# Attention of the sample streams moved from a stage of its own into the two gate projections

## The chip, the cores and the metric

The kernel runs on one core of one Trainium2 chip, written in Bass with every semaphore set by hand. The metric is device time in microseconds from start to end of one execution.

## The reference, cut to what matters

One layer of a hybrid encoder: half-step feed-forward, a token mixer, half-step feed-forward, final norm. There are 1024 tokens of one new stream (prompt) and 8 running streams of 16 new tokens (sample), so T = 1152 tokens of width 1024. The mixer is what changes:

```
xr, gr, q, k, v, fl, ga, gb = split(h @ w_in)
a_out = gelu(gr) * rg_lru(causal_conv(xr))
logf  = log_sigmoid(fl + b_fgt)
att   = attend(q, k, v, logf)     # prompt: causal. sample: over cache and new tokens
z = sigmoid(ga) * (a_out @ w_br_rnn) + sigmoid(gb) * (att @ w_br_att)
x = x + (1 + gate) * (z @ w_out)

def fox_sample(...):              # 8 streams, 16 heads of 64, 1024 cached rows + 16 new
    s = einsum('bqhd,bkhd->bhqk', q, kk) * HEAD_DIM ** -0.5
    s = s + ft[query] - ft[key]   # ft: running sums of logf, past ones and new
    return einsum('bhqk,bkhd->bqhd', softmax(where(mask, s, -inf)), vv)
```

The outputs are the tokens after the layer, and the new keys, values, logf and states.

## The kernel before, in words

Each engine has its own program, a row of stages: setup, first feed-forward, projection (`proj_*`), recurrent branch (`brr_*`), prompt attention (`att_*`), sample attention (`sat_*`), merge of the branches and output projection (`merge_*`), second feed-forward, final norm. Loops are hardware loops (`Fori`) whose bodies are written out in full; the first and last passes are often written out ahead of and behind the loop.

A product of full precision is three fp32r passes (`mm3`, L273 to L277): weights and activations are each split into a high part (ScalarE, L257, and a cast) and the remainder (GpSimd, L263, for weights). A weight block is 1024 x 256. SyncE loads it, ScalarE and GpSimd split it, TensorE uses it for six groups (two tiles of 128 outputs, three chunks of 384 tokens); a group is eight steps over k of three matmuls into one PSUM bank. `PROJ_SLOTS` and the like say which buffers a block takes and how many blocks ago they were used last.

The projection has four iterations of seven blocks, for the columns xr, gr, q, k, v, ga, gb; groups rotate over six banks, which ScalarE empties. Between the groups of v and ga, TensorE turns keys and values to token rows (L1109) for the outputs. Between those of q it does the small products of the recurrence gates (L1132), whose recurrence VectorE computes. Gate values and q, k, recurrent output go to DRAM. The recurrent branch loads its 4.7 MB input at once, splits it in three chunks (ScalarE L1438, VectorE L1453) and starts.

The sample attention (`sat_*`) has 16 units, a stream times half of the heads, eight heads in four pairs. For one unit: load 2 MB of cached keys (`kc`) and 2 MB of values (`vc`), biases (`sp`, eight DMAs of 65 KB), new queries and keys in a scattered pattern of 16 tokens (`qd`, `kn`, L1730 and L1731). For each head pair, 8 transposes of keys (L1771) into banks 6 and 7, copies to `kTs` (ScalarE L1845, VectorE L1882), then two products of the pair's 32 query rows with 512 keys each (L1784). A pair writes 32 partitions of the score banks. Then new-token scores (L1792, L1794), reduction with the biases (L1888), Exp (L1849), nine transposes (L1804), copies (L1856, L1858, L1901), 36 products with the values (L1815) in rotation over the four pairs, scaling (L1904), a transpose (L1821), and the hi/lo split into the activations (L1917, L1921). Two units overlap: scores of the next one stand before the finish of the last one. The prompt attention ends with transposes at L1561; the merge starts with `mm3` matmuls as soon as the attention is in the activations.

Of the kernel before, what the change touches and what calls it, by code (L numbers as in the profile page):

```python
# [35 lines left out]
CH = 384  # L36
# [22 lines left out]
def program(nc, ctx, a, o):  # L59
# [101 lines left out]
    gate_p = sb(rnnf, "gate_p", [128, 2, 3])  # L161
    rnnf.close()
    brrf = ExitStack()
    a_stage = sb(brrf, "a_stage", [128, KT, T])
    state_out = sb(brrf, "state_out", [36, D])
    lf16 = sb(brrf, "lf16", [ST, 128])
    brrf.close()
    projf.close()
    set2.close()

# [24 lines left out]
    satf = ExitStack()  # L195
    NEWK = PAST // 128
    kc = [sb(satf, f"kc{n}", [128, NEWK, 512]) for n in range(2)]
    vc = sb(satf, "vc", [128, NEWK, 512])
    kTs = [sb(satf, f"kTs{n}", [128, PAST]) for n in range(2)]
    kn = [sb(satf, f"kn{n}", [128, 4, ST]) for n in range(2)]  # L200
    vn = [sb(satf, f"vn{n}", [ST, 512]) for n in range(2)]
    qd = [sb(satf, f"qd{n}", [128, 4, 2 * ST]) for n in range(2)]
    sp = [sb(satf, f"sp{n}", [128, PAST + ST]) for n in range(2)]
    spT = sb(satf, "spT", [128, NEWK + 1, 128])
    sstat = sb(satf, "sstat", [128, 2, 4])
    o_rows = sb(satf, "o_rows", [128, 128])
    satf.close()


# [16 lines left out]
    N_PROJ = 28  # L226
    B_BRR = B_PROJ + N_PROJ
# [5 lines left out]
    PROJ_SLOTS = [(0, 1, 2, 3), (1, 2, 0, 2), (0, 2, 1, 3), (1, 2, 2, 3), (0, 2, 0, 3), (1, 2, 1, 3), (0, 2, 0, 2)]  # L233
    BRR_SLOTS = [(0, 1, 2, 3), (1, 2, 1, 3), (0, 2, 0, 3), (1, 2, 1, 2)]
# [5 lines left out]
    BRR_RAWS = (PROJ_RAWS[0] + 16, PROJ_RAWS[1] + 12)  # L240
# [228 lines left out]
    def setup_tensor(eng):  # L469
# [5 lines left out]
        eng.sem_inc(sem("sa_sc"), 5)  # L475
# [568 lines left out]
    COLS = (COL_XR, COL_GR, COL_Q, COL_K, COL_V, COL_GA, COL_GB)  # L1044
    XR, GR, Q, K, V, GA, GB = range(7)
    ST_BEFORE = {Q: 0, K: 1, V: 2, GA: 2, GB: 3}
# [6 lines left out]
    def proj_sync(eng):  # L1053
        w_in_v = kview(a["w_in"][0])

        def load(i, j):
            load_block(eng, B_PROJ + i * 7 + j, PROJ_SLOTS[j], w_in_v[:, :, ds(i * 256 + COLS[j], 256)])

# [14 lines left out]
        for j in range(2, 7):  # L1073
            load(0, j)
        with eng.Fori(1, N_IT) as i:
            load(i, 0)
            eng.wait_ge(sem("ri_full"), i * 12)
            load_gates(i)
            for j in range(1, 7):
                load(i, j)  # L1080

    def proj_tensor(eng):
# [9 lines left out]
        def body(i, first):  # L1092
            for j in range(7):
                for n in range(6):
                    t, c = n // 3, n % 3
                    g = i * 42 + j * 6 + n
# [610 lines left out]

    UNITS = 2 * SB  # L1710

    def sat_sync(eng):

# [456 lines left out]
```

## Time and profile before

| | |
|---|---|
| three runs | 3626.4, 3628.4, 3630.88 us, median 3628.4 |
| profiled execution | 3627.85 us, span 3625.7 us, mean TensorE clock 0.975 |
| TensorE busy | 3439.9 us, 95% of the span |
| VectorE, ScalarE, GpSimd busy | 1283.6, 910.2, 704.2 us |
| DMA | 343.2 MB, mean 95 GB/s |

The span runs from the first instruction to the last. A busy TensorE need not be at its full rate: the granted clock is 1.00 or 0.50, and 32-row products run side by side or not while both count as busy. In the timelines a run of instructions of one line is merged into one row with its start, its length and its count; the last instruction of a run overlaps the next run, so starts are to be compared and not ends. An fp32 product is recorded as two matmuls, a transpose as one.

### The profile page before, as it was taken

What the parts mean: (1) busy time and instruction counts of PE and PEld (TensorE: products, weight loads), DVE (VectorE), ACT (ScalarE), POOL (GpSimd) and SP (SyncE); (2) the same over time, 40 slices, a digit from 0 to 9 for tenths busy, and PEclk for the clock granted to TensorE, in tenths of its full rate; (3) what the DMA queues carried; (4) which work ended last, traced back from release to release, by engine and by line L of the source; (5) the groups of instructions that cost most, each with busy time, mean ns of one, the idle gap of its engine ahead of it and who ended that gap; (6) DMA issues with size and microseconds to landing.
All of it is one profiled execution on the core that took longest, in us unless ns stands there. A gap on an engine that the chain in (4) does not pass through costs nothing.

```text
span 3625.7 us, 54412 instructions
## 1 busy us (share of the span) xinstructions
PE 3439.9 (95%) x21295; PEld 3232.4 (89%) x21295; DVE 1283.6 (35%) x2835; ACT 910.2 (25%) x1360; POOL 704.2 (19%) x283
## 2 busy tenths in 40 slices
PE   5999999999999999999988998888999999999997
PEld 3999999999889999999988886445998999999996
DVE  5322222233364141414116775332415322233225
ACT  3111111111233232323216663221113111111112
POOL 1222222222112112112212220000122222232220
PEclk7999999999999999999999999998999999999999
DMA  6232222221112222122443435997310111111101
GB/s 207 82 104 93 93 93 81 81 93 36 76 39 93 82 88 88 65 99 72 168 143 95 98 88 155 279 277 251 123 47 27 44 58 35 35 43 38 58 12 52
DMA packets 264224, 343.20 MB, mean 95 GB/s; under 512 B 56381, under 2 KB 201205, under 8 KB 263858
## 3 DMA queue, kind: packets, MB, share of 16 engines
q1 hardware_dynamic: 237682, 308.42, 27.4%
q10 hardware_dynamic: 26432, 33.18, 2.6%
q8 instruction: 86, 1.41, 0.2%
q14 instruction: 24, 0.20, 0.0%
HBM read 293.54 MB, written 48.01 MB: 94 GB/s over the span
## 4 chain that ended last, share of the span: by engine, by line
PE 88%; DVE 4%; DMA 3%; issue 2%; ACT 2%; SPq 1%; DVEq 0%; ACTq 0%
PE psum L273 25%; PE psum L277 25%; PE psum L276 24%; PE psum L1554 3%; DMA kn<-k_t 2%; PE psum L1784 2%; PE psum L1534 2%; PE psum L1771 1%; PE psum L455 1%; DVE h_f L660 1%; PE psum L1132 1%; PE psum L1521 1%; PE psum L1815 1%; SPq L1738 1%; PE psum L1522 1%
## 5 line engine op out<-in xcount | busy, mean ns | idle before, releaser
L273 PE MATMUL psum<-acts_hi,w_hi 128*128 128x384 f32 x4032 | 1375.9, 341 | 50.3 <-DVE past_rows L309 25.2
L277 PE MATMUL psum<-acts_hi,w_lo 128*128 128x384 f32 x4032 | 1358.7, 337 | 0.0
L276 PE MATMUL psum<-acts_lo,w_hi 128*128 128x384 f32 x4032 | 1358.4, 337 | 0.0
L273 PEld LDWEIGHTS psum<-acts_hi,w_hi 128*128 128x128 f32 x4032 | 762.0, 189 | 71.6 <-issue 56.0
L263 POOL TENSOR_TENSOR w_lo<-w_raw,w_hi 128x2048 fp32r<-128x2048 f32 x106 | 492.1, 4650 | 1628.5 <-ACT w_hi L257 1628.5
L276 PEld LDWEIGHTS psum<-acts_lo,w_hi 128*128 128x128 f32 x4032 | 762.3, 189 | 3.3
L277 PEld LDWEIGHTS psum<-acts_hi,w_lo 128*128 128x128 f32 x4032 | 761.6, 189 | 0.0
L938 DVE TENSOR_TENSOR u_f<-psum,gated 128x384 f32<-128x384 f32 x132 | 73.6, 557 | 1045.2 <-ACT gated L884 1045.2
L971 DVE SCALAR_TENSOR_TENSOR x<-psum,mods,x 128x384 f32<-128x384 f32 (+1 forms) x552 | 314.6, 570 | 190.7 <-PE psum L277 190.7
L257 ACT ACTIVATE w_hi<-w_raw 128x2048 fp32r<-128x2048 f32 x106 | 200.6, 1911 | 639.7 <-PE psum L273 605.3
L273 PE MATMUL psum<-u_hi,w_hi 128*128 128x384 f32 x1056 | 355.3, 336 | 0.0
L277 PE MATMUL psum<-u_hi,w_lo 128*128 128x384 f32 x1056 | 354.9, 336 | 0.0
L276 PE MATMUL psum<-u_lo,w_hi 128*128 128x384 f32 x1056 | 354.7, 336 | 0.0
L907 POOL TENSOR_TENSOR u_lo<-u_f,u_hi 128x384 fp32r<-128x384 f32 x132 | 134.2, 1016 | 941.5 <-ACT u_hi L886 941.5
L884 ACT ACTIVATE gated<-psum 128x384 f32<-128x384 f32 x132 | 64.8, 491 | 914.8 <-PE psum L277 914.8
L273 PEld LDWEIGHTS psum<-u_hi,w_hi 128*128 128x128 f32 x1056 | 198.5, 188 | 0.3
L276 PEld LDWEIGHTS psum<-u_lo,w_hi 128*128 128x128 f32 x1056 | 198.5, 188 | 0.3
L277 PEld LDWEIGHTS psum<-u_hi,w_lo 128*128 128x128 f32 x1056 | 198.5, 188 | 0.0
L1554 PE MATMUL psum<-vh,pT 128*128 128x64 f32 x1152 | 147.2, 274 | 9.0 <-DVE acts_lo L1675 6.3
L1554 PEld LDWEIGHTS psum<-vh,pT 128*128 128x128 f32 x1152 | 141.4, 195 | 13.1 <-DVE acts_lo L1675 9.2
L1187 ACT ACTIVATE st<-psum 128x384 f32<-128x384 f32 x120 | 58.9, 491 | 334.3 <-PE psum L277 333.3
L1601 ACT ACTIVATE pr<-pr,stat 128x128 f32<-128x128 f32 (+7 forms) x128 | 98.8, 772 | 51.1 <-DVE stat L1655 50.0
(231 smaller groups left out, 2842.9 us busy)
## 6 DMA issues: line engine op xcount, KB each, us to landing
w_raw<-in_ffn_w SPq DMA_DIRECT2D x66, 1024.0 KB, 5.3
kc<-in_cache_k SPq DMA_DIRECT2D x16, 2048.0 KB, 10.9
vc<-in_cache_v SPq DMA_DIRECT2D x16, 2048.0 KB, 9.1
w_raw<-in_w_ada SPq DMA_DIRECT2D x28, 1024.0 KB, 5.0
w_raw<-in_w_in SPq DMA_DIRECT2D x28, 1024.0 KB, 5.2
sp<-sample_bias SPq DMA_DIRECT2D x128, 65.0 KB, 6.9
ada_w<-in_w_ada SPq DMA_DIRECT2D x4, 2048.0 KB, 15.5
w_raw<-in_w_ada_f SPq DMA_DIRECT2D x8, 1024.0 KB, 5.5
```

The lines of the kernel that those rows point to most:

```text
L257: eng.activation(w_hi[st][:], w_raw[raw][:], ACT.Copy).then_inc(sem("w_hi_done"), 1)
L263: eng.tensor_tensor(w_lo[st][:], w_raw[raw][:], w_hi[st][:].bitcast(F32), ALU.subtract).then_inc(sem("w_lo_done"), 1)
L273: pass1 = eng.matmul(out, whi, ahi, start=first, stop=False)
L276: eng.matmul(out, whi, alo, start=False, stop=False)
L277: return eng.matmul(out, wlo, ahi, start=False, stop=last)
L907: eng.tensor_tensor(u_lo[:, t, tokens_of(c)], u_f[n % 2][:], u_hi[:, t, tokens_of(c)].bitcast(F32), ALU.subtract).then_inc(sem("u_lo_done" ...
L938: eng.tensor_tensor(u_f[n % 2][:], ps[2 * (n % 2) + 1][:, 0:CH], gated[n % 2][:], ALU.mult).then_inc(sem("u_free"), 1)
L971: last = eng.scalar_tensor_tensor(xt[:, d, t0:t0 + cp], bank[:, 0:cp], mods[:, gate, d, 0:1], xt[:, d, t0:t0 + cp], ALU.mult, ALU.add)
L1534: last = eng.transpose(ps[4 + kb // 4][:, 128 * (kb % 4):128 * (kb % 4) + 128], pr[k % 4][:, 128 * kb:128 * kb + 128], ident[:])
L1554: last = eng.matmul(ps[6 + k % 2][:, 0:HD], pT[k % 2][:, 128 * kb:128 * kb + 128], vh[hh][:, kb, :], start=(kb == 0), stop=(kb == qi))
L1601: eng.activation(pr[k % 4][:, 0:keys], pr[k % 4][:, 0:keys], ACT.Exp, bias=stat[:, k % 4, 1:2], accum_out=stat[:, k % 4, 2:3]).then_inc(se ...
L1784: last = eng.matmul(psum[rows, base + 512 * bk:base + 512 * bk + 512], qd[g][:, p, :], kTs[p % 2][:, 512 * bk:512 * bk + 512], start=True, ...
```

## The change

- The projection keeps five blocks an iteration (xr, gr, q, k, v), with new buffer slots. Its value transposes move from the ga block to the xr block of the next iteration.
- The eight gate blocks (ga, gb of each quarter) become a stage of their own, `mix_*`, with 48 groups rotating over four banks. The other four banks are for the sample attention: three for scores, weighted values and output, one (`TURNED`) for turned keys.
- The 16 units are cut into pieces, 12 slots each. Three groups make a window; a slot comes every two k steps. In a window TensorE does slots 0 to 3 (turn keys of the first 512 rows, a head pair each), 4 and 5 (turn the last unit's probabilities), 6 (scores of the first half, four pairs one behind another), 7 to 10 (turn the second half's keys; slot 7 also the weighted values of the last unit, slot 9 its output transpose), 11 (scores of the second half, new tokens). The last body holds five windows in its twelve groups, with a slot every 1.5 steps.
- Keys, values, scores and biases have one buffer each, keys loaded in halves. `sp` and `spT` are single. Queries and new keys of all units are loaded once (`qs`, `kns`) and copied into place by GpSimd. ScalarE and VectorE share the key copies one by one.
- The attention goes to `att_s` and is split into the activations beside the prompt attention. The new tokens' offsets (`lf16`, `new_f`) are computed at the start of the new stage.
- The recurrent branch's input is loaded in three chunks and its first two are split behind the last groups. `sat_*` goes.

The core of the diff (the projection's part is the renumbering of blocks and waits from seven to five):

```
-    PROJ_SLOTS = [(0, 1, 2, 3), (1, 2, 0, 2), (0, 2, 1, 3), (1, 2, 2, 3), (0, 2, 0, 3), (1, 2, 1, 3), (0, 2, 0, 2)]
+    PROJ_SLOTS = [(0, 1, 2, 2), (1, 2, 1, 2), (0, 2, 0, 3), (1, 2, 2, 3), (0, 2, 1, 3)]
+    WINDOWS = 4
+    SLOTS = 12
+    def slots_of(n, last):
+        steps = [s * 3 // 2 if last else 2 * s for s in range((WINDOWS + last) * SLOTS)]
+        return [s for s, at in enumerate(steps) if 8 * n <= at < 8 * n + 8], steps
...
+        def window(i, w, begin=False, end=False):          # SyncE, mix_sync
+            u, b, g, _ = unit_of(i, w * SLOTS)
+            _, b1, g1, _ = unit_of(i, (w + 1) * SLOTS)
+            if w == 0:
+                load_block(eng, B_MIX + 2 * i + 1, ...)
+            if w == 2 and not end:
+                load_block(eng, B_MIX + 2 * i + 2, ...)
...
+            if not last_unit:
+                eng.wait_ge(sem("sa_kt"), u * 8 + 4)
+                keys(b1, g1, 0)
+            if not begin:
+                eng.wait_ge(sem("sa_pt"), u * 2)
+                bias(b, g)
+                eng.wait_ge(sem("sa_pv"), u)
+                values(b, g)
+            if not last_unit:
+                eng.wait_ge(sem("sa_kt"), u * 8 + 8)
+                keys(b1, g1, 1)
...
+            new_values(b, g)
...
+        def turn_keys(u, x, first):                        # TensorE, mix_tensor
+            half, p = x // 4, x % 4
+            if p == 0:
+                eng.wait_ge(sem(f"kc_loaded{half}"), u * 16 + 16)
+            if not (first and x == 0):
+                eng.wait_ge(sem(("sa_kev_v", "sa_kev_a")[x % 2]), u * 4 + (x + 1) // 2)
+            for m in range(4):
+                last = eng.transpose(ps[TURNED][:, 128 * m:128 * m + 128], kc[:, 4 * half + m, 128 * p:128 * p + 128], ident[:])
+            last.then_inc(sem("sa_kt"), 1)
+        def scores(u, g, half, first):
+            eng.wait_ge(sem("sa_kev_a"), u * 4 + 2 * half + 2)
+            eng.wait_ge(sem("sa_kev_v"), u * 4 + 2 * half + 2)
...
+            for p in range(4):
+                last = eng.matmul(psum[32 * p:32 * p + 32, base + 512 * half:base + 512 * half + 512], qd[g][:, p, :],
+                                  kTs[:, p, :], start=True, stop=True)
...
+        def piece(i, s, first, last):
+            if keys and at < 4:
+                turn_keys(u, at, first and s < SLOTS)
+            if done and at == 4:
+                turn_probs(u - 1, (0, 1, 2, 3, 8))
+            if done and at == 5:
+                turn_probs(u - 1, (4, 5, 6, 7))
+            if keys and at == 6:
+                scores(u, g, 0, first and s < SLOTS)
+            if keys and at >= 7 and at < 11:
+                turn_keys(u, at - 3, False)
+            if done and at == 7:
+                weighted(u - 1)
+            if done and at == 9:
+                turn_out(u - 1)
+            if keys and at == 11:
+                scores(u, g, 1, False)
+                new_scores(u, g, first and s < SLOTS)
+        def body(i, first=False, last=False):
+            for n in range(12):
+                here, steps = slots_of(n, last)
...
+                if first and n < 3:
+                    turn_tokens(eng, 12 * N_IT - 6 + 2 * n, 2 * n, 5)
+                    turn_tokens(eng, 12 * N_IT - 6 + 2 * n + 1, 2 * n + 1, 5)
...
+                for k in range(KT):
+                    for s in here:
+                        if steps[s] == 8 * n + k:
+                            piece(i, s, first, last)
+                    opens = mm3(eng, ps[n % 4][:, 0:CH], ...)
...
+        def piece(i, s, first, last):                      # ScalarE, mix_scalar
+            if keys and at in (0, 2, 7, 9):
+                eng.activation(kTs[:, x % 4, :], ps[TURNED], ACT.Copy).then_inc(sem("sa_kev_a"), 1)
+            if done and at == 1:
+                eng.activation(sp[:], sp[:], ACT.Exp, ...).then_inc(sem("sa_exp"), 1)
+            if done and at == 4:
+                eng.activation(spT[0:ST, NEWK, :], psum[0:ST, base + 1024:base + 1152], ACT.Copy)
+            if done and at == 5:
+                eng.activation(spT[:, 4:8, :], ...).then_inc(sem("sa_pe_a"), 1)
+        def body(i, first=False, last=False):
+            for n in range(12):
+                if first and n < 3:
+                    move_tokens(eng, N_IT - 1, 1, 2 * n, 5)
+                    move_tokens(eng, N_IT - 1, 1, 2 * n + 1, 5)
+                for s in here:
+                    piece(i, s, first, last)
+                eng.activation(st[t][:, tokens_of(c)], ps[n % 4][:, 0:CH], ACT.Sigmoid).then_inc(sem("proj_free"), 1)
+                if c == NC - 1:
+                    eng.dma_start((ga_dram, gb_dram)[j][...], st[t][:])
+                if n == 1:
+                    split_hi(eng, B_MIX + 2 * i + 1, ...)
+                if n == 7:
+                    split_hi(eng, B_MIX + 2 * i + 2, ...)
+                if last and n >= 9:
+                    a_hi(eng, n - 9)
...
+        def body(i, first=False):                          # GpSimd, mix_gpsimd
+            for w in range(WINDOWS):
+                if not (first and w < 2):
+                    eng.wait_ge(sem("sa_sc"), u * 2 - 2)
+                eng.tensor_copy(kn[g][:], kns[:, 4 * g:4 * g + 4, toks])
+                for half in range(2):
+                    eng.tensor_copy(qd[g][rows, :, ST * half:ST * half + ST], qs[rows, 4 * g:4 * g + 4, toks])
+                if w % 2 == 1:
+                    split_lo(eng, B_MIX + 2 * i + 1 + w // 2, PAIR_SLOTS[1 - w // 2])
...
+        def piece(i, s, first, last):                      # VectorE, mix_vector
+            if keys and at in (1, 3, 8, 10):
+                eng.tensor_copy(kTs[:, x % 4, :], ps[TURNED]).then_inc(sem("sa_kev_v"), 1)
+            if done and at == 4:
+                eng.tensor_copy(spT[:, 0:4, :], ...).then_inc(sem("sa_pe_v"), 1)
+                eng.reciprocal(old[:, 3:4], old[:, 2:3])
+            if done and at == 8:
+                eng.tensor_scalar(o_rows[:], psum[:, base + 1280:base + 1408], old[:, 3:4], None, ALU.mult)
+            if done and at == 10:
+                output(i, s // SLOTS - 1, u)
+            if keys and at == 11:
+                eng.tensor_tensor_reduce(sp[:], psum[:, base:base + PAST + ST], sp[:], 1.0, -3e38, ALU.add, ALU.max, new[:, 0:1])
+                eng.tensor_scalar(new[:, 1:2], new[:, 0:1], -1.0, None, ALU.mult).then_inc(sem("sa_neg"), 1)
...
+    def a_hi(eng, c):
+        eng.wait_ge(sem(f"a_loaded{c}"), 16)
+        eng.activation(acts_hi[:, :, tokens_of(c)], a_stage[c][:], ACT.Copy).then_inc(sem("a_hi"), 1)
...
     def att_scalar(eng):
+        eng.wait_ge(sem("br_full"), 24)
+        eng.activation(acts_hi[:, :, TP:T], att_s[:], ACT.Copy).then_inc(sem("sa_hi"), 1)
```

## Rows read from the trace of the kernel before

**Rows 1.** The page: busy tenths of TensorE in 40 slices of the span.
```profile
PE   5999999999999999999988998888999999999997
```

**Rows 2.** By stage: window, length, busy of each engine, clock, DMA share, GB/s.
```profile
1403.00:1592.00 189.00, 186.41 (x1062) 182.48 (x1062) 57.77 (x58) 57.85 (x85) 32.42 (x7) 1.00 0.25 84
...
2228.00:2515.00 287.00, 241.81 (x2224) 137.64 (x2224) 98.58 (x240) 70.36 (x128) 0.00 (x0) 0.93 0.87 262
```

**Rows 3.** The chain of waits in the sample attention: start, length, what.
```profile
2369.80 9.62 DMA kn<-k_t
```

**Rows 4.** Timeline of TensorE at both ends of the sample attention.
```profile
2223.02 0.47 PE L1561 MATMUL psum<-ident,att 128*128 128x128 f32 x1 [0.23 <-DVE att L1664]
...
2513.83 0.33 PE L1821 MATMUL psum<-ident,o_rows 128*128 128x128 f32 x1 [0.55 <-DVE o_rows L1904]
2515.20 0.44 PE L273 MATMUL psum<-acts_hi,w_hi 128*128 128x384 f32 x1 [1.04 <-DVE acts_lo L1921]
```

**Rows 5.** TensorE at the recurrent branch's start; then that stretch by windows.
```profile
1778.69 0.34 PE L277 MATMUL psum<-acts_hi,w_lo 128*128 128x384 f32 x1
1786.70 0.66 PE L273 MATMUL psum<-acts_hi,w_hi 128*128 128x384 f32 x1 [7.67 <-issue]
...
1786.50:1795.00 8.50, 8.30 (x33) 8.33 (x34) 7.19 (x4) 5.84 (x3) 3.38 (x1) 0.66 0.68 220
```

**Rows 6.** Timeline of TensorE in one unit of the sample attention.
```profile
2386.11 1.90 PE L1784 MATMUL psum<-kTs,qd 128*32 128x512 f32 x4
2387.95 1.09 PE L1771 MATMUL psum<-ident,kc 128*128 128x128 f32 x8
2388.97 2.30 PE L1784 MATMUL psum<-kTs,qd 128*32 128x512 f32 x8
2391.20 0.27 PE L1792 MATMUL psum<-causal_r,pick_r 16*128 16x16 f32 x1
...
2391.59 1.20 PE L1804 MATMUL psum<-ident,sp 128*128 128x128 f32 x9
2393.84 1.95 PE L1815 MATMUL psum<-vc,spT 128*32 128x128 f32 x64 [1.04 <-DVE spT L1901]
...
2396.07 1.10 PE L1771 MATMUL psum<-ident,kc 128*128 128x128 f32 x8
```

**Rows 7.** Timeline of TensorE around three transposes in the projection.
```profile
1129.09 0.49 PE L1109 MATMUL psum<-ident,st 128*128 128x128 f32 x3
...
1129.60 0.34 PE L276 MATMUL psum<-acts_lo,w_hi 128*128 128x384 f32 x1
...
1129.94 0.34 PE L273 MATMUL psum<-acts_hi,w_hi 128*128 128x384 f32 x1
```

**Rows 8.** Timelines of ScalarE and VectorE: key copies, Exp, a table load.
```profile
2396.85 0.60 ACT L1845 ACTIVATE kTs<-psum 128x512 f32<-128x512 f32 x1 [3.74 <-PE psum L1771]
...
2399.38 1.16 ACT L1849 ACTIVATE sp<-sp,sstat 128x1040 f32<-128x1040 f32 x1 [0.51 <-DVE sstat L1891]
...
2399.37 0.69 DVE L1882 COPY kTs<-psum 128x512 f32<-128x512 f32 x1
...
1157.69 1.28 ACT L1187 ACT_TABLE_LOAD   x1 [0.49 <-ACT tok L1218]
```

**Rows 9.** The chain at the projection loop's back edge, and the iteration around it by windows.
```profile
1396.15 2.49 issue
...
1215.00:1403.00 188.00, 184.98 (x1047) 181.05 (x1046) 57.75 (x58) 57.37 (x84) 32.45 (x7) 0.99 0.26 85
```

**Rows 10.** DMA of the sample attention (2228 to 2530): share, KB each, landing time.
```profile
q1 hardware_dynamic: 54299, 79.96, 86.9%
...
vc<-in_cache_v SPq DMA_DIRECT2D x16, 2048.0 KB, 9.1
kc<-in_cache_k SPq DMA_DIRECT2D x15, 2048.0 KB, 10.9
...
w_raw<-in_w_br_att SPq DMA_DIRECT2D x1, 1024.0 KB, 13.9
```

More of the change, by code:

```diff
@@ L192, in program @@
     patf.close()
[L195 to L207, printed above, removed]
     zf = ExitStack()
@@ L1078, in proj_sync @@
             load_gates(i)
-            for j in range(1, 7):
+            for j in range(1, NJ):
                 load(i, j)
@@ L1136, in proj_tensor, with turn_tokens @@
             body(i, False)
+    def turn_tokens(eng, e, n, bank0):
+        t, c = n // 3, n % 3
+        eng.wait_ge(sem("tok_moved"), e + 1)
+        for m in range(3):
+            last = eng.transpose(ps[bank0 + n % 2][:, 128 * m:128 * m + 128],
+                                 st[t][:, CH * c + 128 * m:CH * c + 128 * m + 128], ident[:])
+        last.then_inc(sem("tok_turned"), 1)
     def logf_turn(eng):
@@ L1158, in proj_scalar, with body @@
         log1p_scalar(eng, rt[1][0:H, :], FL_STEP)
-        def body(i, first):
-            for j in range(7):
+        def body(i, first, last=False):
+            for j in range(NJ):
                 for n in range(6):
                     t, c = n // 3, n % 3
-                    g = i * 42 + j * 6 + n
+                    g = i * 6 * NJ + j * 6 + n
                     tile = i * 2 + t
-                    if j in (V, GA):
-                        move_tokens(eng, i, j, n)
+                    if j == V:
+                        move_tokens(eng, i, 0, n, 6)
+                    if j == XR and not first:
+                        move_tokens(eng, i - 1, 1, n, 6)
                     eng.wait_ge(sem("proj_full"), g + 1)
@@ L1206, in proj_scalar, with move_tokens @@
         body(0, True)
-        with eng.Fori(1, N_IT) as i:
+        with eng.Fori(1, N_IT - 1) as i:
             body(i, False)
-    def move_tokens(eng, i, j, n):
+        body(N_IT - 1, False, last=True)
+    def move_tokens(eng, i, which, n, bank0):
         t, c = n // 3, n % 3
-        which = j - V
         e = i * 12 + which * 6 + n
@@ L1254, in proj_gpsimd @@
         split_lo(eng, B_PROJ, PROJ_SLOTS[0])
-        with eng.Fori(0, N_IT) as i:
-            for j in range(7):
-                split_lo(eng, B_PROJ + i * 7 + j + 1, PROJ_SLOTS[(j + 1) % 7])
+        with eng.Fori(0, N_IT - 1) as i:
+            for j in range(NJ):
+                split_lo(eng, B_PROJ + i * NJ + j + 1, PROJ_SLOTS[(j + 1) % NJ])
+        for j in range(1, NJ):
+            split_lo(eng, B_PROJ + (N_IT - 1) * NJ + j, PROJ_SLOTS[j])
+        split_lo(eng, B_MIX, MIX_FIRST_SLOT)
     class Steps:
@@ L1358, in brr_sync @@
         for t in range(2):
             eng.wait_ge(sem(f"a_stored{t}"), (N_IT + 1) * 16)
-        eng.dma_start(a_stage[:], kview(a_dram)).then_inc(sem("a_loaded"), 16)
+        eng.wait_ge(sem("past_stored"), 32)
+        bias(0, 0)
+        for w in range(WINDOWS):
+            window(0, w, begin=(w == 0))
+        with eng.Fori(1, N_IT - 1) as i:
+            for w in range(WINDOWS):
+                window(i, w)
+        for w in range(WINDOWS):
+            window(N_IT - 1, w, end=True)
+        a_rows = kview(a_dram)
```

571 lines of the change are left out of this document (301 added, 270 removed).

## The prediction

> **What bounds the kernel now.** I read the page first: the busy times (TensorE 95% of the 3625.7 us span) and the slices [rows 1]. TensorE stands at 9 tenths nearly everywhere, with a dent at slices 25 to 28. So time can only go by taking TensorE work away, by filling its idle time, or by running its work at the full clock. The table by stage then says where the dent is [rows 2]: a projection iteration (1403 to 1592) is 98.6% busy, while the sample attention (2228 to 2515) has TensorE busy 242 of 287 us, a granted clock of 0.93, and the DMA engines at 87% and 262 GB/s. The chain of waits inside it names the limit [rows 3]: in every second unit TensorE waits for `kn<-k_t`, a scattered load of new keys that takes 9.6 us to land.
>
> **What goes.** (a) The stage runs from the last transpose of the prompt attention at 2223.02 to the first merge matmul at 2515.20 [rows 4], 292.2 us. The hand-over from one to the other stays; between the last transpose of this stage and the merge it takes 1.4 us. **-290.8**. (b) Before the recurrent branch TensorE waits for the hi/lo split of its input, 1778.69 to 1786.70, and then runs at a mean clock of 0.66 for 8.5 us [rows 5]: 7.8 + 8.5 x 0.34 = 10.7 us. In the change the input comes in three chunks, and chunks 0 and 1 are split behind the last two gate groups (4.2 us each, against 2.8 us for a ScalarE pass). Chunk 2 is loaded once the last unit's weighted values are done, some 7 us before the end; at the 9 us of a load of that kind it is split 8 us into the branch, which asks for it at 8.3 us. That is no margin; I take the whole gain, **-10.7**, and keep 4 us for the range.
>
> **What comes in its place**, per unit (16 of them), from starts on TensorE [rows 6]. Keys: 32 transposes. A transpose put between projection matmuls costs 0.11 us and no switch: 1129.09 to 1129.60 holds three and one matmul, and two matmuls take 0.34 [rows 7]: 32 x 0.11 = 3.5. Scores: today one head pair's two halves take 1.84 (2386.11 to 2387.95), since both write the same 32 output partitions and queue up; the last two pairs, adjacent, take 2.23 together (2388.97 to 2391.20), so different groups of output columns do overlap; and the weighted values, four groups in rotation, take 2.23 for 36 products. Now four pairs follow one another, once for each half: 2 x (0.86 + 0.09) = 1.9, where today it is 2 x 1.84 + 2.23 = 5.9. New tokens 0.4 (2391.20 to 2391.59), nine probability transposes 1.0, weighted values 2.2 (2393.84 to 2396.07), output transpose 0.2. Sum 9.2 us a unit, **+147**. Bounds of the scores: 0.9 a half (all four at once) and 4 x 0.92 a half (none), which would be +88 on the total; I take the near end because the 36 products show four groups together.
> The Trainium skill, TensorEngine Tiling (Array Packing), section Tiling Modes, says that a change of tiling mode drains the engine, which speaks against strewing 32-column products between full-width ones. The trace agrees in kind: the first start after a scores run is about 0.09 us late; by this rule the switches of term (c) are paid, and by the row of three transposes, which stay full-width, they would be nothing.
>
> (c) Each piece sits alone between matmuls. A first transpose after a wait is about 0.06 us longer than the next, and four more changes between narrow and full products at 0.09 are not in the rows above: 0.7 us a unit, **+11**. Bounds 0 [rows 7] and 20.
>
> (d) Stalls of the interleaving. A gate group is 24 matmuls, 4.16 us; a window is three groups and one unit, with a slot every 6 matmuls (1.04 us). I walk it. Only one bank takes turned keys, so each turn waits for the copy of the one before: 0.40 us from the last of four transposes to the copy's start (the run that starts at 2396.07 has its fourth about 0.39 later, and ScalarE copies from 2396.85), 0.60 on ScalarE or 0.69 on VectorE [rows 6, 8], and 0.06 back: 1.06 or 1.15. The cover is 0.11 + 1.04. It just fits where the copying engine is free. VectorE is (reduction 1.23, copies 0.69, about 7 of 23 us). ScalarE is in order: at a window's start it first does the sigmoid (0.49) and issues the gate store (0.35), so the first key copy ends at 1.8 us and slot 1 waits 0.4. Then it reloads the table for Exp (1.28) and does the exponentials (1.16 + 0.19) to 4.5; the copy behind them ends at 5.1 and slot 3 waits 0.3. The second load, for the sigmoid, starts before its wait for TensorE, as in [rows 8] (right behind a move, 3 us ahead of its sigmoid), and is hidden. The weight split (1.92) behind a sigmoid holds up slot 10 by 0.2 in every second window. Sum 0.75 us, x 12 windows: **+9**.
> The Trainium skill, ScalarE: Activation LUTs, section Table sets, puts exp and sigmoid in different sets, and its section on what a table load costs gives about 2.7 us. The trace has 1.28 for the load [rows 8]; by the page's figure the exponentials would end 1.4 us later and the sum grow by 22 us.
>
> (e) The last body packs five windows into twelve groups: every second slot has 0.52 us of cover instead of 1.04, so four or five turns a window wait 0.5 to 0.6: 4 x 2.7, and the tail window about 1: **+12**. (f) The first window: TensorE waits for the last eviction (0.8), ScalarE has two row stores and six token moves (0.49 + 0.38 each) ahead of its key copies, and GpSimd's query copies wait for the store of `a_t`: **+5**, bounds 1 and 12. GpSimd's small copies are not in the trace; they lie between nothing and 2 us each, and have a window of cover. (g) A long loop body costs at its back edge: in the projection ScalarE's last eviction and then 2.49 us of issue [rows 9], 3.0 in all, and a clock of 0.99 over the 188 us around it adds some 1.9: 5 us. The new loop has one back edge on each engine: **+6**. (h) ScalarE casts 1024 columns ahead of the first exponentials of the prompt attention: **+1**.
>
> At nothing: the projection with five blocks. Its VectorE chain ends, by the 57.8 us a iteration holds of it, well inside the 138 us that remain (188 less two blocks of 25); the value transposes move one block later under the same cover. The score offsets, once computed at the end of the recurrent branch, now lie behind the first groups.
>
> **The sum**: -290.8 - 10.7 + 147 + 11 + 9 + 12 + 5 + 6 + 1 = -110.5. The span falls from 3625.7 to 3515; the profiled execution took 3627.85 around it, 2.2 more, so 3517 us. That execution is within 0.6 us of the median of the three runs, 3628.4.
>
> **The DMA check.** The stage now moves 80 MB in 302 us at 86.9% of the engines [rows 10], 305 GB/s at full share, with the small packets of the new-token loads among them, which go. The interleaved stage (48 gate groups 200 us + 191 = 391) moves some 101 MB: caches 67, biases 8.5, weights 8.4, gate stores 9.4, the branch input 4.7, the rest 3. That is 258 GB/s, 85% of what the rows show. In order of issue: keys' first half at slot 3 for the next window (17 us early, lands within 11), biases at slot 5 for slot 11 (eight at 0.5 us, then 6.9, against 13), values at slot 7 for the next slot 7, keys' second half at slot 10 for the next slot 7 (14 us). All fit, none by much more than double.
>
> **Rivals.**
> 1. The turn-copy-turn loop misses by a little everywhere: cover and round trip on VectorE are both 1.15 us. With 0.3 us lost at each of 8 turns: 16 x 2.4 = +38, **3555**. For: both copying engines are in order and shared. Against: the rows that I walked had it fit.
> 2. The DMA binds. If the mix of loads and stores reaches only 240 GB/s, 101 MB take 421 us, not 391: **3547**. For: 87% share already. Against: the small packets go.
> 3. It does better: ScalarE's work hides, chunk 2 is early, no slot waits. Without (c), (d) and half of (e), (f): **3489**.
> 4. Slower than before: SyncE issues the loads in order, each behind progress of TensorE. If each ended only before the next began, a window would be keys 10.9 + biases 3.9 + 6.9 + values 9.1 + half a weight block of 13.9, so 7: 37.8 us against 23.1: 16 x 14.7 = +235, **3752**. It decides from 30 us a window, 6.9 over mine. Against: issues wait for TensorE, not for landings, and the slots put them 5 to 9 us apart.
> 5. The change doesn't do what it says for the scores, no overlap at 512 columns: +88, **3605**.
>
> **How the numbers follow.** Forecast 0.56, rival 1 0.16, rival 2 0.11, rival 3 0.11, rival 4 0.03, rival 5 0.03. The likeliest gives 3517. The low end takes rival 3; the high end takes rivals 1 and 2 with the scores' or the first window's bounds on top: 3488 to 3566. About 7 us (0.2%) is what a measurement of this kernel tells from no change. Faster: all but rival 4 and a mix of 5 with others, 0.95; same 0.01; slower 0.04.
>
> **What would show it.** Right: no stretch without gate matmuls between the prompt attention and the merge; four score products starting within some 10 ns and 0.9 to 1 us a half; a window of 23 to 24 us; TensorE's clock at 1.00 through the stage but for one dip at the back edge; the recurrent branch starting within 1 us of the last gate group. Wrong: waits of TensorE on `kTs` copies over 1 us a window (rival 1), waits on `kc` or `vc` loads (rivals 2 and 4), one score product at a time (5), or a clock under 1.00 in the loop, which no term above has.

## The result, and the profile after

The changed kernel takes 3504.6 us (median; 3501.5 to 3507.9) against 3627.5 us for the kernel before: a ratio of 0.966, interval 0.9643 to 0.9677. It is faster by 123 us, or 3.4%. The forecast was 3517, inside a range of 3488 to 3566. The profiled execution took 3501.9 us and its span is 3499.8 us, so the span fell by 125.9 where -110.5 was predicted.

The page first: the busy time of TensorE and the tenths of its busy time, of the granted clock and of the DMA engines, in 40 slices of 87.5 us.

```profile
PE 3356.5 (96%) x21295; PEld 3194.3 (91%) x21295; DVE 1275.1 (36%) x2801; ACT 946.1 (27%) x1390; POOL 716.0 (20%) x334
...
PE   5999999999989999999999989999999999999997
...
PEclk7999999999999999999999999999999999999998
DMA  6223222221122231247767634334111111111101
```

The dent of slices 25 to 28 [rows 1] is gone. The DMA load, which stood at 0.87 in one stage [rows 2], now lies at 6 to 7 tenths over slices 19 to 23.

The table by stage, columns as in [rows 2]: the projection (four bodies of five blocks), the whole mixed stage with the branch's start, six undisturbed windows of it, the window with the loop's back edge, and the branch behind it.

```profile
1018.00:1563.20 545.20, 545.14 (x3087) 527.16 (x3087) 250.80 (x245) 190.91 (x281) 92.83 (x20) 1.00 0.26 87
1563.20:1963.00 399.80, 378.89 (x3445) 317.34 (x3445) 100.75 (x214) 161.02 (x227) 47.79 (x58) 0.99 0.74 248
1588.20:1726.70 138.50, 136.97 (x1268) 114.79 (x1267) 33.40 (x79) 55.42 (x81) 17.25 (x19) 1.00 0.75 254
1726.70:1757.30 30.60, 22.98 (x213) 18.95 (x211) 6.12 (x16) 8.92 (x14) 1.21 (x6) 0.94 0.72 248
1963.00:2055.00 92.00, 92.00 (x535) 91.85 (x534) 12.27 (x22) 10.53 (x8) 23.23 (x6) 1.00 0.45 145
```

The windows of the mixed stage have TensorE busy 98.9% of the time at full clock; the stage of before had 84% at 0.93 [rows 2]. What is still idle stands in the fourth row: 7.6 us at the back edge. The projection is busy 545.14 of 545.20 us, where an iteration of before had 2.6 us idle [rows 2].

Where the 125.9 us of span came from, by starts on TensorE:

| stretch | before | after | difference |
|---|---|---|---|
| set-up and first feed-forward | 1021.7 | 1018.1 | -3.7 |
| projection blocks | 757.1 | 545.1 | -212.0 |
| 48 gate groups with sample attention | none | 391.5 | +391.5 |
| gap and half clock at the branch's start | 10.7 | 0 | -10.7 |
| recurrent branch | 102.0 | 101.5 | -0.5 |
| prompt attention | 331.5 | 332.2 | +0.7 |
| sample attention by itself | 292.2 | none | -292.2 |
| hand-over to the merge | | 1.2 | +1.2 |
| merge on | 1110.5 | 1110.2 | -0.3 |

The sum is -126.0, within 0.1 of the span's difference. Of the projection's -212.0, 199.7 are only moved: 48 gate groups of 24 matmuls at 0.1733 us, which the next row holds again.

The timeline of TensorE in one window shows the new weave: start, length, engine, line, operation, tiles, count.

```profile
1603.91 0.60 PE L1497 MATMUL psum<-ident,kc 128*128 128x128 f32 x4
...
1605.42 0.60 PE L1497 MATMUL psum<-ident,kc 128*128 128x128 f32 x4
...
1607.02 0.60 PE L1497 MATMUL psum<-ident,kc 128*128 128x128 f32 x4
...
1608.62 1.07 PE L1511 MATMUL psum<-kTs,qd 128*32 128x512 f32 x8
1609.62 0.27 PE L1520 MATMUL psum<-causal_r,pick_r 16*128 16x16 f32 x1
...
1610.00 0.45 PE L288 MATMUL psum<-acts_hi,w_hi 128*128 128x384 f32 x1
```

Four transposes stand every 1.5 to 1.6 us with six gate matmuls between. The eight score records (two for each of the four products) take 1.00 us from the first start to the next operation's: 0.99 to 1.0 us for four head pairs, where one pair's two halves took 1.84 [rows 6]. The overlap on which the forecast put much of its gain, and which rival 5 denied, is there.

ScalarE's and VectorE's timelines in the same window show the order that was walked in term (d): sigmoid, store of the gates, key copy, table load, exponentials, key copy, table load back.

```profile
1611.38 0.49 ACT L1646 ACTIVATE st<-psum 128x384 f32<-128x384 f32 x1 [4.72 <-PE psum L292]
1611.90 0.34 ACTq L1649 DMA_DIRECT2D gate_a_t<-st  x1
1612.34 0.60 ACT L1618 ACTIVATE kTs<-psum 128x512 f32<-128x512 f32 x1 [0.47 <-ACT st L1646]
1612.95 1.28 ACT L1622 ACT_TABLE_LOAD   x1
1614.25 1.16 ACT L1622 ACTIVATE sp<-sp,sstat 128x1040 f32<-128x1040 f32 x1
...
1615.41 0.58 ACT L1618 ACTIVATE kTs<-psum 128x512 f32<-128x512 f32 x1
1616.00 1.28 ACT L1646 ACT_TABLE_LOAD   x1
1617.79 0.49 ACT L1646 ACTIVATE st<-psum 128x384 f32<-128x384 f32 x1 [0.50 <-PE psum L292]
```

```profile
1613.68 0.69 DVE L1711 COPY kTs<-psum 128x512 f32<-128x512 f32 x1 [2.02 <-PE psum L1497]
```

The second table load starts right behind the copy, 1.79 us before its sigmoid: it is hidden, as the forecast had it. Each load takes 1.28 us. In the last body the slots lie closer, and in its last window the load is not hidden. There TensorE stands still for 2.18 us, until the copy behind the load and the sigmoid has been made:

```profile
1918.83 1.28 ACT L1646
1920.12 0.49 ACT st L1646
1920.61 0.50 ACT kTs L1618
...
1921.15 0.66 PE psum L1497 x4
```

By the forecast's figure from the Trainium skill (ScalarE: Activation LUTs, section What ACT_TABLE_LOAD costs) of about 2.7 us, an estimated 22 us would have been added over the stage. The windows of the first three bodies, but for the first and the two behind the back edge, are 22.95 to 23.25 us, so that did not come.

The chain of waits at the back edge of the mixed loop:

```profile
1747.24 0.99 PE psum L1511 x8
...
1750.43 6.83 issue
1757.27 1.11 PE psum L1497 x4
```

6.83 us in which TensorE waited for nothing that the profile shows; in the projection of before it was 2.49 [rows 9]. The end of the stage, on TensorE, where before there were 8 us between two such rows [rows 5]:

```profile
1954.49 0.33 PE L292 MATMUL psum<-acts_hi,w_lo 128*128 128x384 f32 x1
1954.66 0.33 PE L288 MATMUL psum<-acts_hi,w_hi 128*128 128x384 f32 x1
```

### The profile page after: what moved, and what is told of

Same layout as the page of the kernel before. It is cut to its first block, busy times and chain, and to the rows that moved or that the text cites. A ratio compares the mean times of both kernels' runs of the same rounds, so it can differ in the third digit from the quotient of the medians.

```text
span 3499.8 us, 54119 instructions
## 1 busy us (share of the span) xinstructions
PE 3356.5 (96%) x21295; PEld 3194.3 (91%) x21295; DVE 1275.1 (36%) x2801; ACT 946.1 (27%) x1390; POOL 716.0 (20%) x334
## 4 chain that ended last, share of the span: by engine, by line
PE 90%; DVE 4%; ACT 3%; issue 2%; DMA 1%; ACTq 0%; SPq 0%; DVEq 0%
PE psum L288 26%; PE psum L292 25%; PE psum L291 25%; PE psum L1934 3%; PE psum L1914 2%; PE psum L1497 1%; PE psum L470 1%; PE psum L1544 1%; DVE h_f L674 1%; PE psum L1511 1%; PE psum L1146 1%; PE psum L1901 1%; PE psum L1902 1%; DVE psum L669 1%; ACT acts_hi L715 1%
## 5 line engine op out<-in xcount | busy, mean ns | idle before, releaser
L288 PE MATMUL psum<-acts_hi,w_hi 128*128 128x384 f32 x4032 | 1390.0, 345 | 35.0 <-DVE past_rows L324 23.5
L1934 PEld LDWEIGHTS psum<-vh,pT 128*128 128x128 f32 x1152 | 142.1, 196 | 12.3 <-DVE acts_lo L2060 8.6
L1711 DVE COPY kTs<-psum 128x512 f32<-128x512 f32 x64 | 44.3, 692 | 247.1 <-PE psum L1497 247.1
```

Of the source, the lines that this page charges most:

```text
L288: pass1 = eng.matmul(out, whi, ahi, start=first, stop=False)
L1934: last = eng.matmul(ps[6 + k % 2][:, 0:HD], pT[k % 2][:, 128 * kb:128 * kb + 128], vh[hh][:, kb, :], start=(kb == 0), stop=(kb == qi))
```

## The experiments

Ratios are to the kernel before, measured on the same chip. The runs were made on three chips, with medians of the kernel before of 3626.2, 3625.5 and 3624.1 us.

**The changed kernel again.**

> The changed kernel itself, beside the next three on one chip, so that they can be compared with it. 3505 us, within 4 either way.

3504.9 us (3504.1 to 3506.5), ratio 0.967 (0.9657 to 0.9683). The differences below are taken to this figure, unless said otherwise. Its interval is some 5 us either way, so a difference of a few us is read from the traces and not from the medians.

**The scores alone, in the kernel before.** Four head pairs' halves are turned and then scored together, but in the stage of its own:

```
-            turn(0)
-            for p in range(4):
-                if p < 3:
-                    turn(p + 1)
...
+            for x in range(6):
+                turn(x)
+            for half in range(2):
...
+                for p in range(4):
+                    last = eng.matmul(psum[32 * p:32 * p + 32, base + 512 * half:base + 512 * half + 512], qd[g][:, p, :],
+                                      kTs[:, p, :], start=True, stop=True)
```

> The kernel before, sample attention still a stage of its own, but with four head pairs' keys turned and then scored (half of the keys at a time): one part of the change alone. Theory: four products side by side save 4.0 us a unit on TensorE, but the stage is near the DMA's pace (87% share), and the copies are no longer all hidden (a unit goes from 10.6 to about 8.5 us up to its scores). At most 2.1 x 16 = 34 us; the DMA leaves at most 25. Time 3600 to 3618, and the waits for the new keys grow. Rival: the grouping is worth its full 64 us wherever it stands: 3563. Other rival: no overlap at 512 columns: 3627 or slower.

3636.0 us (3629.3 to 3639.4), ratio 1.0032 (1.0018 to 1.0045): 0.3% slower than before, where 10 to 28 us less were expected. Its table and its timeline of TensorE:

```profile
2228.00:2515.00 287.00, 205.34 (x2151) 130.89 (x2151) 97.59 (x235) 71.06 (x128) 0.00 (x0) 0.86 0.85 260
```

```profile
2388.74 0.66 PE L1771 MATMUL psum<-ident,kc 128*128 128x128 f32 x4 [0.46 <-ACT kTs L1846]
2390.26 0.66 PE L1771 MATMUL psum<-ident,kc 128*128 128x128 f32 x4 [0.86 <-DVE kTs L1883]
2391.79 1.06 PE L1782 MATMUL psum<-kTs,qd 128*32 128x512 f32 x8 [0.88 <-DVE kTs L1883]
...
2399.92 4.34 PE L1771 MATMUL psum<-ident,kc 128*128 128x128 f32 x20 [2.19 <-DMA kn<-k_t]
```

The overlap works here too (eight records in 1.06 us) and takes 36 us of TensorE work from the same 287 us (205.3 busy, 241.8 before). All of it turned into waits: for the copies, 0.3 to 0.9 us each, and still for the new keys. The granted clock fell with the idle time, 0.86 against 0.93. Two units take 37.6 us (2362.30 to 2399.92) where they took 34.2. So the new order of keys and scores is worth nothing, and a little less, in the old stage. The waits on the new keys' load are as long as before there (20.2 us against 22.7), those on the key copies are new. The changed kernel ends both, with gate matmuls between the turns and with the new keys loaded once for all units; no run tells what either of the two is worth alone.

**Half of the scores pair by pair.** In the changed kernel, the second half's products are put one at a time behind the turns of slots 8 to 10, as soon as each pair's copy is there; the first half stays together:

```
-            for p in range(4):
+            for p in range(4) if half == 0 or first else (3,):
...
+            if keys and at >= 8 and at < 11 and not (first and s < SLOTS):
+                pair_scores(u, g, at - 8)
```

> The changed kernel with the second half's keys scored pair by pair, in slots 8 to 11, right behind each pair's turning; the first half stays four at once. Theory: alone a product takes 0.86 us and two changes of width at 0.09, so three of the four no longer hide: 3 x (0.86 + 0.1 to 0.2) = 3.0 us a unit, 15 units, 45 us more, 3550. Rival: the products cost the same wherever they stand (no overlap in the changed kernel): 3508. Partial overlap: between.

3555.6 us (3551.2 to 3562.2), ratio 0.9807 (0.9792 to 0.9822): +50.7, or 3.4 us a window (26.4 to 26.6). Its timeline of TensorE shows one product alone and four together:

```profile
1615.00 1.04 PE L1511 MATMUL psum<-kTs,qd 128*32 128x512 f32 x2
...
1627.15 1.06 PE L1511 MATMUL psum<-kTs,qd 128*32 128x512 f32 x8
```

One costs as much as four. Three more runs of 0.9 to 1.04 a window are 2.7 to 3.1. The switches between narrow and full products may make the rest; that wasn't taken apart. The price of the scores' order is 3.4 us a half, and by estimate twice that, about 7 us, for both halves of a unit.

**The turns one step apart.** In the two middle bodies the slots follow after one k step (three matmuls, 0.52 us) instead of two:

```
-        steps = [s * 3 // 2 if last else 2 * s for s in range((WINDOWS + last) * SLOTS)]
+        steps = [s * 3 // 2 if last else 2 * s if first else s // SLOTS * 24 + s % SLOTS for s in range((WINDOWS + last) * SLOTS)]
```

> The changed kernel with the slots of a window one k step apart instead of two in the two middle bodies (8 windows): pieces in the first twelve steps, gate matmuls alone in the other twelve. The work is the same. Theory (term d): a turn then has 0.52 us less cover than its 1.06 to 1.15 us round trip, so some six turns a window wait about 0.55 us each, and the exponentials are no longer covered (2 us at slot 4): 5 us a window, 8 windows, 40 us more, 3545. Rival: TensorE's sum alone sets the time, the spacing is not needed: 3505.

3526.0 us (3522.2 to 3530.4), ratio 0.9733 (0.9718 to 0.9747): +21, about half of the +40 expected, with dense windows of 25.7 to 25.9 us. By the trace the eight windows cost 21 us and the back edge gives some 6 back (its gap is 2.79 us here, see the quarter of the loads). Its timeline of TensorE:

```profile
1688.24 0.66 PE L1497 MATMUL psum<-ident,kc 128*128 128x128 f32 x4 [0.95 <-ACT kTs L1618]
...
1689.77 0.66 PE L1497 MATMUL psum<-ident,kc 128*128 128x128 f32 x4 [0.35 <-DVE kTs L1711]
...
1691.29 0.66 PE L1497 MATMUL psum<-ident,kc 128*128 128x128 f32 x4 [0.33 <-ACT kTs L1618]
```

These turns keep 1.52 us apart, with three gate matmuls between them instead of six: 0.38 us up to the start of the last transpose, then a round trip of 1.14 us through the one bank and its copy. Half the cover leaves waits of 0.33 to 0.35 us at three turns and at the scores, and one of 0.95 where ScalarE does something else first. I had priced the exponentials as exposed too; they stay covered.

**A second bank for the turned keys.** Turns alternate between two banks, and the gate groups rotate over three instead of four; the waits and VectorE's and ScalarE's reads follow:

```
-                last = eng.transpose(ps[TURNED][:, 128 * m:128 * m + 128], kc[:, 4 * half + m, 128 * p:128 * p + 128], ident[:])
+                last = eng.transpose(ps[TURNED - x % 2 * 4][:, 128 * m:128 * m + 128], kc[:, 4 * half + m, 128 * p:128 * p + 128], ident[:])
...
-                    opens = mm3(eng, ps[n % 4][:, 0:CH], whi[k], wlo[k], acts_hi[:, k, tokens_of(c)],
+                    opens = mm3(eng, ps[n % 3][:, 0:CH], whi[k], wlo[k], acts_hi[:, k, tokens_of(c)],
```

> Turned keys alternate between two PSUM banks, the gate groups rotate over three instead of four; each turn then waits for the copy before the last. Theory (term d: one bank, a round trip of 1.06 to 1.15 us against as much cover): slot 1 of each window no longer waits its 0.33 us, and the last body loses some 1.2 us a window: 15 x 0.33 + 4 x 1.2 = 10 us less than the changed kernel, 3495. Rival: what holds slot 1 is TensorE's own restart after a semaphore wait, or three gate banks are too few: no change, or slower.

3491.2 us (3488.1 to 3493.6), ratio 0.9633 (0.9619 to 0.9646): -13.7. Its full windows are 22.56 us, but for the first and those at the back edge, and those of the last body 20.00. The stretch of the third row above:

```profile
1588.20:1726.70 138.50, 138.50 (x1289) 119.34 (x1289) 34.31 (x80) 58.33 (x86) 17.77 (x21) 1.00 0.77 259
```

TensorE does not wait once in it. So the stalls of the changed kernel on its one bank are 0.4 to 0.7 us in a full window, 1.2 to 1.8 in the first three windows of the last body and 3.0 in the last one, with the 2.18 us above. Some 1 to 2 us of the 13.7 are not stalls on the bank: the gap at the back edge is 5.13 us here, for 7.37 and 7.89 in the two traces of the changed kernel. And a unit with nothing to wait for costs 22.56 - 12.48 (72 matmuls at 0.1733 us) = 10.08 us, which (unit work and (c) together) was forecast as 9.9.

**The mixed loop written out.** TensorE's loop over the two middle bodies becomes straight code:

```
-        with eng.Fori(1, N_IT - 1) as i:
+        for i in range(1, N_IT - 1):
```

> Only TensorE's loop over the two middle bodies of the new stage is written out. Theory: the 7.7 us gap at that loop's back edge is TensorE fetching its code again, and it halves the clock for the 6.8 us behind it. Written out, the code is fetched ahead: the gap of 6.8 us of issue goes, and with it 3.4 us of slow clock, so 10 us less than the changed kernel, 3495. Rival: the gap is waiting for ScalarE's or VectorE's own back edge, which stays; then nothing changes (3505) and the gap stands in the same place with another releaser.

3499.2 us (3494.6 to 3504.7), ratio 0.9656 (0.9642 to 0.9669): -5.7, with an interval that reaches from about -10 to 0. By the traces of this run and of the changed kernel again, the back edge itself is worth more: its window falls from 31.14 to 23.12 us and the next from 24.68 to 23.45, -9.2. TensorE goes on there without a gap.

But its first window is 2.4 us longer (25.68 against 23.3). The chain of the changed kernel again, then that of this one, tells where:

```profile
1574.03 5.21 DMA out_v_sample<-tok
```

```profile
1574.45 8.14 DMA out_v_sample<-tok
```

ScalarE waits for a store of token rows to land, 5.2 us in the one and 8.1 in the other. Why that store is later when TensorE's code is longer isn't settled.

**Both.** The second bank and the written-out loop together.

> Both edits together. If both theories hold they add up, since one is at the back edge and the other inside the windows: 20 us less, 3485. If either fails, its part is missing.

3483.4 us (3478.1 to 3486.3), ratio 0.9605 (0.9592 to 0.9618): the fastest version, 21.5 us under the changed kernel, about the sum of the two differences (19.4). Its window where the back edge was has no idle time left, beside the 7.6 us above:

```profile
1726.70:1757.30 30.60, 30.60 (x266) 27.21 (x266) 8.73 (x20) 13.39 (x20) 2.19 (x7) 1.00 0.78 264
```

**A quarter of the cached keys and values.** After the first unit only one of four rows of the key halves and two of eight of the values are loaded, so the attention is computed on stale rows. This takes the DMA load away and nothing else:

```
-            rows = slice(4 * half, 4 * half + 4)
+            rows = slice(4 * half, 4 * half + 1)
...
-            eng.dma_start(vc[:], v_rows[:, ds(b * 8, 8), 512 * g:512 * g + 512]).then_inc(sem("vc_loaded"), 16)
+            eng.dma_start(vc[:, 0:2, :], v_rows[:, ds(b * 8, 2), 512 * g:512 * g + 512]).then_inc(sem("vc_loaded"), 16)
```

> The changed kernel with only a quarter of each unit's cached keys and values loaded after the first unit (the rest of the buffers keep the first unit's rows): some 48 MB less. The computation is as long. Theory: the DMA binds nowhere in the new stage (258 GB/s of about 305), so the windows stay at 23.0 to 23.2 us. If the code fetch at the back edge is slow because the DMA engines are busy with bulk loads, the 7.7 us gap shrinks to the 3 us of the old projection: 3505 less 4 or 5 and some clock, 3498. If the fetch is slow for another reason: 3505. If the DMA binds: much less, the windows shorter.

3501.8 us (3499.2 to 3504.3), ratio 0.9663 (0.965 to 0.9676). Six windows and the chain at the back edge:

```profile
1588.00:1726.00 138.00, 136.48 (x1265) 114.34 (x1265) 32.89 (x79) 55.42 (x81) 16.57 (x18) 1.00 0.38 120
```

```profile
1750.44 2.90 issue
1753.33 1.11 PE psum L1498 x4
```

With 120 GB/s instead of 254 the windows are the same to 0.1 us: no load or store binds, and rival 2 falls. Only the back edge is shorter, 2.90 us for 6.83, and its window takes 27.8 us for 31.6. The medians are 3.1 us apart, which their intervals alone would not tell from nothing.

The DMA records say why. In the changed kernel, the queue of TensorE's code between 1750 and 1762:

```profile
q8 instruction: 3, 0.05, 1.4%
```

and in this one, in the same stretch:

```profile
q8 instruction: 3, 0.05, 1.7%
```

Three pieces of 16 KB in both, beside the loads and stores; with TensorE's loop written out no piece is fetched at that place. The gap is a fetch of the loop's first instructions, and its length depends on when the first piece gets its turn. In the changed kernel that piece starts to move at 1754.38, 4.5 us behind TensorE's last matmul; here it starts at 1750.45, 0.5 us behind it. From there to TensorE's next start it is 2.9 us in both. Over the eleven back edges in the traces of all kernels this last part is 2.7 to 3.2 us, while the gap goes from 2.6 to 7.9.

So the mean rate isn't what counts. The kernel with turns one step apart moves 234 GB/s (1660 to 1750), and its chain has only this at the back edge:

```profile
1764.36 2.25 issue
```

Its last bulk load was issued 7.4 us before the edge, that of the changed kernel 1.9 us before. That the code waits for loads issued shortly before is read from these times; no run moves one load alone.

**No early split.** The branch's input is rounded only after the last gate group, as before (its wait is for the last group too):

```
-                if last and n >= 9:
-                    a_hi(eng, n - 9)
...
     def brr_scalar(eng):
+        for c in range(NC):
+            a_hi(eng, c)
```

> The changed kernel with the recurrent branch's input split only after the last gate group, as before. Theory (term b): TensorE waits for one ScalarE and one VectorE pass again, 2.8 + 3.4 + latencies, 7 us, and runs slow for some 8 us behind it: 10 us more than the changed kernel, 3515. Rival: the new stage leaves a wait there anyway, or the clock does not fall: 3508 or less.

3516.4 us (3507.4 to 3525.5), ratio 0.9698 (0.9681 to 0.9715): +11.5, some 6 either way. Its timeline of TensorE at the branch's start, then that stretch:

```profile
1967.29 0.66 PE L288 MATMUL psum<-acts_hi,w_hi 128*128 128x384 f32 x1 [7.25 <-issue]
```

```profile
1967.20:1975.70 8.50, 8.41 (x35) 8.44 (x36) 7.08 (x3) 3.81 (x2) 3.30 (x1) 0.68 0.66 216
```

The gap of 7.4 us and the clock of 0.68 for 8.5 us behind it are back: 7.4 + 8.5 x 0.32 = 10.1, the size and the two parts of term (b).

**The kernel before with its projection loop written out.** One line, as in the mixed loop: `with eng.Fori(1, N_IT)` becomes a plain `for`.

> The kernel before, with only TensorE's projection loop (three iterations of seven blocks) written out. Theory: the 12 us that the projection gained beyond the forecast are its two back edges, gone because a body of five blocks stays in the instruction buffer. Written out there is no back edge in the kernel before either: two gaps of 2.8 us and two stretches of 3.4 us at half clock go, 9 us less than the kernel before, 3618. Rival: the gain came from something else of the five-block body (fewer loads, other slots), and this changes nothing: 3627.

3617.3 us (3610.8 to 3621.2), ratio 0.9976 (0.9967 to 0.9985): 8.7 us less than the kernel before by the ratio, 5 to 12 by its interval. The three iterations that the loop ran have no gap:

```profile
1025.00:1765.00 740.00, 740.00 (x4226) 725.27 (x4225) 250.25 (x244) 236.40 (x345) 129.77 (x28) 1.00 0.27 90
```

The kernel before lost this at its two back edges, gaps of 3.0 and 2.6 us and 3.4 us at half clock behind each. The change lost it no longer, without any loop written out (below).

## Why the prediction was right

**(a), the old stage goes.** -290.8 forecast; -292.2 + 1.2 = -291.0 measured. [rows 4] gave it outright.

**(b), the branch's start.** -10.7 forecast, and all of it came: the gap is gone and the clock stays at 1.00. Taking the early split out gave back 11.5. The split of chunk 2, which had no margin on paper, was not late: TensorE is busy 92.00 of the 92 us from 1963.

**The unit's work and (c).** 9.9 forecast, 10.08 measured. The scores' term, by far the widest, came out at the near end: 0.99 us for four products of 512 columns. (The forecast's 0.86 stands in none of its rows; with the 0.09 behind it, 0.95, it came near.) The half scored pair by pair gives the other end on the chip. That difference, some 7 us a unit, was the real risk of the forecast. [rows 6] had pointed the right way with two pairs of 512 columns and four groups of 128; four groups at 512 columns were shown only by the runs.

**(d) and (e), the stalls.** 9 and 12 forecast; about 6 and 7 measured, from windows of 22.95 to 23.25 against 22.56, and of 21.15 to 21.79 and a last one of 22.96 against 20.00. The mechanism was right: it is the round trip over one bank, shown by the second bank, which removes it all, and by the dense slots, which raise it from some 0.6 to 3.3 us a window. The walk let every ScalarE delay through to TensorE; some were covered. It missed the one in the last window, where the table load for the sigmoid stands in the way.

**(f), the first window.** 5 forecast; 4 to 5 measured, and the row that holds it up is ScalarE's wait for a token store, which the forecast had only as queued stores.

**(g), the back edge.** 6 forecast from [rows 9], 8.3 measured (30.6 us for the window, 24.05 for the next, against 23.1). In the second trace of the changed kernel it is 9.4. It was mis-sized by 2 to 3 because the term was taken from a loop in which the code's first piece moved 0.25 us behind the last matmul; here it moved 4.5 us behind. The prompt attention, for which (h) forecast 1, is 0.7 longer.

Together the mixed stage was forecast at 391 us and took 391.5, closer than its terms were, and that is luck: (d) and (e) were too large by 8, the unit's work was too small by 16 x 0.18 = 2.9 and (g) by 2.3, and 2.0 of value turns had moved in. The rest, some 2 us of the first and last windows, is not apportioned.

**The step that failed** is the first under "At nothing": "the projection with five blocks". It gave 12.3 us more than the moved groups. 5.6 of them are the gaps of two back edges and 3.4 what the half clock behind them costs (two stretches of 3.4 us), and writing out the same loop in the kernel before gave 8.7. Another 2.0 are six turns of value tokens that now run in the mixed stage (an estimate from 18 transposes at 0.11 us); some 1 us is not accounted for. I had counted a back edge as the price of every loop. In the queue of instruction fetches the two kernels differ. Before, in an iteration (1215 to 1390):

```profile
q8 instruction: 8, 0.13, 0.3%
```

After, in a stretch of 286 us with two back edges (1274 to 1560), that queue does not appear at all; only another one does:

```profile
q14 instruction: 3, 0.02, 0.0%
```

So a body of five blocks (some 1550 TensorE records: matmuls and weight loads) stays where it is, and one of seven blocks (some 2140) was fetched anew every time. The Trainium skill, Runtime: NRT & Kernel Launch, section Instruction fetch mechanics, states room for 2048 instructions on TensorE, refilled in blocks of 256, and that a taken branch to a place outside the current two blocks stalls on a fetch. The traces agree with the block's size (three pieces, 0.05 MB) and, for these two loops, with the 2048. They don't agree with two blocks: the body of five blocks of weights took six pieces of code in its first pass of the loop (1154 to 1274) and then none. Nor do they fit as simply for the mixed body: with some 1680 records it is under 2048 too and is fetched again. Written out it takes seven pieces (1659 to 1752), the body of seven blocks eight or nine. The records leave out branches and register work, so the count isn't the whole; what tips it between six pieces and seven is open.

The remaining 3.7 us lie ahead of the first projection, in code that the change doesn't touch: the profiled execution of before had one more stretch of 6.8 us at half clock there (116 to 123). That is not a gain of the change: the second trace of the changed kernel has half a stretch of it again (3.4 us from 118). It is in the profiled executions; how much of it is in the medians isn't known.

**The rivals.** 1 (every turn misses) would need 2.4 us a unit; there are 0.4 to 0.7. 2 (DMA) fell with a quarter of the loads. 3 (better, 3489) came nearest of the rivals in time, but not in mechanism: slots do wait. It is about what the second bank makes real, 3491. 4 (serial loads, 37.8 us a window) is refuted by the windows and by landings of 6.3 us for a key half and 7.8 for values. 5 (no overlap) is refuted by four products in 0.99 us, where one alone takes 1.04.

## What to carry to other kernels

Work taken from an engine is worth only what the next wait leaves: 36 us less TensorE work made the old stage slower, while the same order is part of a change that saved 3.4%, with independent matmuls as long as the copy's round trip between the turns. When such cover just fits, a second PSUM bank is worth more than a finer walk of it (-13.7 us for a few lines). Look at the instruction fetches at a hardware loop's back edge, and make the body smaller or write it out where the engine has no other idle time.

## What the runs showed that was not expected

- The wait at a back edge is 2.7 to 3.2 us from the moment at which the first piece of code moves, plus what that piece waits for its turn: 4.5 us in the changed kernel, 0.5 with a quarter of the loads, nothing in the kernel with turns one step apart, at full loads.
- Whether there is one at all depends on the body: none at some 1550 TensorE records (six pieces of code), one at 1680 (seven) and at 2140. It was worth 9.2 us in the mixed loop and 8.7 in the two edges of the old projection.
- Four products into four groups of 32 output columns, 512 columns each, take 0.99 us, and one alone 1.04: a narrow product by itself wastes three quarters of the time.
- Transposes strewn in fours between gate matmuls left the granted clock at 1.00, 32 of them and nine more for every 72 matmuls. The half clock came behind idle stretches: behind the 7.37 us at the back edge, and in the second trace of the changed kernel also behind the 2.18 us in the last body (3.4 us at half clock from 1923.3). In the first trace the same 2.18 us were followed by no slow stretch, so what such a wait costs in clock isn't the same in every execution.
